# Trunk layer on one core: the experts' outputs are summed in DRAM by accumulating scatters

## The reference, cut to what matters

```python
_, idx = lax.top_k(jnp.where(emask, sel, -jnp.inf), TOP_K)
w = jnp.take_along_axis(scores, idx, axis=-1)
w = w / jnp.sum(w, axis=-1, keepdims=True) * ROUTED_SCALE          # 2.5
def block(args):                                                   # 128 slots of one expert
    tok, g, e = args
    xb = t_pad[tok]
    hb = jax.nn.silu(xb @ wg[e]) * (xb @ wu[e])
    return (hb @ wd[e]) * g[:, None]
out = jnp.zeros((T + 1, D), yb.dtype).at[slot_tok].add(yb.reshape(P, D))
...
return (routed + shared).reshape(B, L, D)
x = x + (gate_f * moe_ffn(h, p))                                   # then rmsnorm(x, g_final)
```

## Time and profile before

| | before |
|---|---|
| median of three runs | 2329.45 us |
| the profiled execution: time, span | 2326.84 us, 2325.0 us |
| PE busy in the span | 1948.6 us (84%) |
| DVE (VectorE), ACT (ScalarE), POOL (GpSimd) busy | 790.7, 330.1, 640.5 us |
| mean granted clock of PE | 0.918 |
| read from and written to HBM | 343.39 MB, 45.47 MB |

### The profile page before, as it was taken

One profiled execution on the slowest core, in us unless ns is written; L12 is line 12 of the kernel. 1 busy time (PEld: TensorE's weight loads), 2 busy tenths in 40 slices (PEclk: granted clock), 3 DMA queues, 4 the chain that ended last, 5 costly groups with the idle time before them and its releaser, 6 DMA issues. The chain is left out here.

```text
span 2325.0 us, 23841 instructions
## 1 busy us (share of the span) xinstructions
PE 1948.6 (84%) x7395; PEld 1099.0 (47%) x7396; DVE 790.7 (34%) x1150; ACT 330.1 (14%) x654; POOL 640.5 (28%) x853
## 2 busy tenths in 40 slices
PE   6999836888852567999998885999999999999965
PEld 3555415888841454555553452444444444444422
DVE  1000182444443962111111582333233232332336
ACT  2000232111114220000000110111111111111100
POOL 0000003333302210000000134455555555555444
PEclk8999957999975788999999977999999999999988
DMA  9442100000000014111114003999988999699656
GB/s 351 173 167 73 58 0 3 1 1 1 1 3 0 0 48 174 58 66 56 64 60 126 28 10 125 311 338 349 356 286 284 338 336 338 229 330 332 236 190 246
DMA packets 207419, 357.27 MB, mean 154 GB/s; under 512 B 24333, under 2 KB 158137, under 8 KB 203778
## 3 DMA queue, kind: packets, MB, share of 16 engines
q1 hardware_dynamic: 176338, 293.22, 36.6%
q0 software_dynamic: 31024, 63.27, 7.6%
HBM read 343.39 MB, written 45.47 MB: 167 GB/s over the span
## 5 line engine op out<-in xcount | busy, mean ns | idle before, releaser
L1853 PE MATMUL ps_gu_b<-we_gu,xgT 128*128 x1120 | 497.9, 598 | 39.9 <-issue 21.8
L1853 PEld LDWEIGHTS ps_gu_b<-we_gu,xgT 128*128 128x128 f32 x1120 | 208.1, 191 | 304.1 <-issue 304.1
L1806 POOL DMA_INDIRECT xg<-h_dram,idx_x x288 | 293.1, 1018 | 109.0 <-issue 109.0
L1276 PE MATMUL ps_logit<-hT_back,w_merge_tiles 128*128 128x512 f32 (+1 forms) x1024 | 284.4, 436 | 19.3 <-DMA w_merge_tiles<-w_merge 19.3
L1879 PE MATMUL ps_y_b<-we_dn,hsT_b 128*128 x560 | 253.2, 594 | 2.8 <-issue 2.8
L1276 PEld LDWEIGHTS ps_logit<-hT_back,w_merge_tiles 128*128 128x128 f32 x1024 | 158.1, 192 | 142.9 <-issue 123.5
L309 PE MATMUL ps_turn_and_in<-hT,w_tiles 128*128 128x512 f32 x704 | 197.8, 441 | 1.2 <-DVE hT L256 1.2
L1962 DVE TENSOR_TENSOR hs_b<-sg_b,ps_gu_b 128x256 f32<-128x256 f32 x70 | 29.4, 421 | 472.5 <-ACT sg_b L1911 451.7
L1879 PEld LDWEIGHTS ps_y_b<-we_dn,hsT_b 128*128 128x128 f32 x560 | 103.3, 190 | 120.8 <-issue 120.7
L309 PEld LDWEIGHTS ps_turn_and_in<-hT,w_tiles 128*128 128x128 f32 x704 | 108.8, 193 | 100.4 <-issue 100.4
L1953 DVE STREAM_TRANSPOSE xgT<-xg 128x1024 f32<-128x1024 f32 x72 | 145.1, 2015 | 15.0 <-DMA xg<-h_dram,idx_x 15.0
(11 more groups left out here) (411 smaller groups left out, 2214.0 us busy)
## 6 DMA issues: line engine op xcount, KB each, us to landing
we_gu<-we_gate SPq DMA_DIRECT2D x64, 1024.0 KB
we_gu<-we_up SPq DMA_DIRECT2D x64, 1024.0 KB
we_dn<-we_down SPq DMA_DIRECT2D x128, 512.0 KB
wmod<-w_mod SPq DMA_DIRECT2D x24, 1024.0 KB, 5.7
w_merge_tiles<-w_merge SPq DMA_DIRECT2D x32, 640.0 KB
w_tiles<-w_mix SPq DMA_DIRECT2D x22, 512.0 KB, 3.4
xg<-h_dram,idx_x POOLq DMA_INDIRECT x288
proj<-w_out SPq DMA_DIRECT2D x1, 4096.0 KB
```

Source lines behind the costliest of these rows:

```text
L1276: pe.matmul(ps_l[:, b, lo:hi], w[:, b, k * P:(k + 1) * P], hT[:, k, lo:hi], start=(k == 0), stop=(k == KD - 1))
L1806: pool.indirect_dma_start(xg[:, b, q, :], None, quarters, bass.IndirectOffsetOnAxis(ap=idx_x[:, b, q:q + 1], axis=0), bounds_check=4 * T - ...
L1853: mm = pe.matmul(ps_gu[:, b, :], xT[:, b, k].rearrange("p q s -> p (q s)"), w_gu[:, bass.ds(half[b], 1), k, :].rearrange("p a n -> p (a n) ...
```

## The change

- A list entry is now a pair: token number and the bits of its weight. Both are scattered at once, 8 bytes a row. The expert stage takes the two apart, turns both by a transpose, and the weight is multiplied in with the second SwiGLU product: a 128 x 1 copy and a multiply of three operands for each block (L1956, L1961).
- `y_dram` (5120 rows) is gone. `sum_dram` has a row per token (640). SP writes the shared expert's part there behind the first weight loads (L1777). A store adds its rows to it: the same scatter with `compute_op=ALU.add`, the row being the token number. Within a block all tokens differ.
- Between blocks they may not, so a store waits until the store of the other buffer has landed: `pool.wait_ge(y_store[1 - b], 16 * (i + b))`. Before the second lap's gathers GpSimd also waits for the shared part.
- The combining stage is `finish_tokens`: five plain loads of the sum, gate, residual, norm. Its outputs use one semaphore for each of two buffers.

```diff
-                            tok_u[:, t:t + 1], None).then_inc(scattered, 16)
+                            entry[:, t, j, :].bitcast(U32), None).then_inc(scattered, 16)
...
-                ch.link(dve.tensor_tensor_scan(end[:], ones[:, 0:N_EXP], cnt[:], 0.0, ALU.mult, ALU.add))
-                ch.link(dve.tensor_sub(base[:], end[:], cnt[:]))
-                take(c(B_ROW), base[:], c(B_EXPERT))
...
+                sp.dma_start(m.sum_dram.rearrange("(t p) d -> p t d", p=P), m.acc).then_inc(shared_out, 16)
                 with sp.Fori(1, n) as i:
                     pair(i)
...
                 def store(b, i, done):
                     for c in range(2):
                         pool.wait_ge(y_half_ok[c][b], i + 1)
+                    pool.wait_ge(y_store[1 - b], 16 * (i + b))
                     pool.wait_ge(pool_done, done)
...
-                    pool.indirect_dma_start(m.y_dram, bass.IndirectOffsetOnAxis(ap=idx_y[:, b, 0:1], axis=0),
-                                            y[:, b, :], None, bounds_check=T * TOP_K - 1, oob_is_err=False
+                    pool.indirect_dma_start(m.sum_dram, bass.IndirectOffsetOnAxis(ap=idx_y[:, b, 0:1], axis=0),
+                                            y[:, b, :], None, bounds_check=T - 1, oob_is_err=False, compute_op=ALU.add
                                             ).then_inc(y_store[b], 16)
                 for b in range(2):
                     gather(b, 0, 2 + 2 * b)
+                pool.wait_ge(shared_out, 16)
...
+                        dve.tensor_copy(w_col[:, b, :], all_w[:, bass.ds(2 * i + b, 1)]).then_inc(w_ok[b], 1)
...
-                        dve.tensor_mul(hs[:, b, :], hs[:, b, :], ps_gu[:, b, FF:]).then_inc(hs_ok[b], 1)
+                        dve.wait_ge(w_ok[b], i + 1)
+                        dve.scalar_tensor_tensor(out=hs[:, b, :], in0=hs[:, b, :], scalar=w_col[:, b, :],
+                                                 in1=ps_gu[:, b, FF:], op0=ALU.mult, op1=ALU.mult).then_inc(hs_ok[b], 1)
...
-def combine(nc, m):
+def finish_tokens(nc, m):
...
+                def residual(t):
+                    dve.wait_ge(moe_in[t], 16)
+                    ch.link(dve.tensor_mul(moe[:, t, :], moe[:, t, :], gate[:, group(t), :]))
+                    dve.tensor_add(m.x[:, t, :], m.x[:, t, :], moe[:, t, :]).then_inc(x_ok, 1)
+
+                dve.wait_ge(vec_in, 48)
+                residual(0)
                 for t in range(NT):
+                    if t + 1 < NT:
+                        residual(t + 1)
                     dve.wait_ge(sq_ok, t + 1)
```

More of the change, by code:

```diff
@@ L1364, in output_and_route @@
         pos_in, pos8, addr = a.sb("pos_in", [P, N_EXP]), a.sb("pos8", [P, NT, 8]), a.sb("addr", [P, NT, 8])
-        addr_u, tok_u = a.sb("addr_u", [P, NT, 8], U32), a.sb("tok_u", [P, NT], U32)
-        none_u = a.sb("none_u", [P, N_EXP * T // P], U32)
+        addr_u = a.sb("addr_u", [P, NT, 8], U32)
+        entry = a.sb("entry", [P, NT, TOP_K, 2])
+        weight = [entry[:, t, :, 1] for t in range(NT)]
+        none_u = a.sb("none_u", [P, 2 * N_EXP * T // P], U32)
         wsum = a.sb("wsum", [P, 1])
@@ L1370, in output_and_route @@
         used, count = a.sb("used_e", [P, N_EXP]), a.sb("count_e", [P, N_EXP])
-        ordinal, pairs, last, offset = (a.sb(n, [P, 1]) for n in ("ordinal", "pairs_e", "last_e", "offset_e"))
+        ordinal, pairs, last = (a.sb(n, [P, 1]) for n in ("ordinal", "pairs_e", "last_e"))
         tab = a.sb("tab", [P, TAB], I32)
@@ L1702, in _ @@
                 ch.link(dve.tensor_copy(m.list_row[:], last[:]))
[L1703 to L1709, removed]
+                for t in range(2, NT):
+                    silu(t)
 def experts(nc, m):
     QW = D // 4
-    NO_ROW = 65536.0
     with Tools(nc, "experts") as a:
@@ L1845, in _ @@
                               start=True, stop=True)
[L1846 removed]
+                pe.transpose(ps_list[:, 1, 0:P], list_f[:], ident)
+                pe.transpose(ps_list[:, 1, P:2 * P], list_w[:], ident).then_inc(list_turn, 1)
                 def lap(i):
@@ L1937, in _ @@
                 for q in range(4):
[L1938 to L1943, removed]
+                    dve.tensor_copy(list_4[:, q], list_u[:, 32 * q:32 * q + 32, 0].unsqueeze(1).to_broadcast([P, 4, 32]))
+                dve.tensor_copy(list_w[:], list_u[:, :, 1].bitcast(F32))
+                dve.tensor_copy(list_f[:], list_u[:, :, 0]).then_inc(list_turn, 1)
                 dve.wait_ge(list_turn, 2)
@@ L1946, in _ @@
                                   ps_list[:, 0, :].rearrange("p (q r) -> p q r", q=4),
-                                  4.0, m.place[:, 1:2], ALU.mult, ALU.add)
-                dve.tensor_scalar(all_y[:, :, 0], ps_list[:, 1, 0:P], m.place[:, 0:1], None, ALU.add
-                                  ).then_inc(list_ok, 1)
+                                  4.0, m.place[:], ALU.mult, ALU.add)
+                dve.tensor_copy(all_w[:], ps_list[:, 1, P:2 * P])
+                dve.tensor_copy(all_y[:, :, 0], ps_list[:, 1, 0:P]).then_inc(list_ok, 2)
                 def turn(b, i):
@@ L1973, in _ @@
                     lap(i)
[L1976 to L1980 removed]
+def finish_tokens(nc, m):
+    with Tools(nc, "finish_tokens") as a:
+        moe = a.sb("moe_sum", [P, NT, D])
         gate = a.sb("gate_f", [P, 2, D])
         gf = a.sb("g_final_b", [P, D])
[L1983 to L1985 removed]
         sq, out = a.sb("sq_f", [P, D]), a.sb("out_f", [P, 2, D])
         ss, rms = a.sb("ss_f", [P, NT]), a.sb("rms_f", [P, NT])
[L1988 to L1991 removed]
+        moe_in, out_store = a.ring("f_moe_in", NT), a.ring("f_out_store", 2)
+        (vec_in, x_ok, ms_ok, sq_ok, rms_ok, out_ok, chain) = a.sems(
+            "f_vec_in", "f_x_ok", "f_ms_ok", "f_sq_ok", "f_rms_ok", "f_out_ok", "f_chain")
         with nc.Block() as block:
@@ L2044, in _ @@
                 ch = Chain(dve, chain)
+                def residual(t):
+                    dve.wait_ge(moe_in[t], 16)
+                    ch.link(dve.tensor_mul(moe[:, t, :], moe[:, t, :], gate[:, group(t), :]))
+                    dve.tensor_add(m.x[:, t, :], m.x[:, t, :], moe[:, t, :]).then_inc(x_ok, 1)
                 dve.wait_ge(vec_in, 48)
-                def diagonals(t):
-                    dve.tensor_mul(diag[:, t % 2], m.const[:, 0:P].unsqueeze(1).to_broadcast([P, ON_PE, P]),
-                                   m.weight[:, t, 0:ON_PE].unsqueeze(2).to_broadcast([P, ON_PE, P])).then_inc(diag_ok, 1)
-                diagonals(0)
-                diagonals(1)
-                for t in range(NT):
-                    acc = m.acc[:, t, :]
-                    for j in range(ON_PE, TOP_K):
-                        dve.wait_ge(got[j], 16 * (t + 1))
-                        dve.scalar_tensor_tensor(out=acc, in0=rows[:, j, :], scalar=m.weight[:, t, j:j + 1],
-                                                 in1=acc, op0=ALU.mult, op1=ALU.add).then_inc(added, 1)
-                        dve.wait_ge(added, t * (TOP_K - ON_PE) + j - ON_PE + 1)
-                    dve.wait_ge(used, (t + 1) * ON_PE)
-                    if t + 2 < NT:
-                        diagonals(t + 2)
-                    dve.tensor_add(acc, acc, ps[:, t % 2, :]).then_inc(summed, 1)
-                    dve.wait_ge(summed, t + 1)
-                    ch.link(dve.tensor_mul(acc, acc, gate[:, group(t), :]))
-                    dve.tensor_add(m.x[:, t, :], m.x[:, t, :], acc).then_inc(x_ok, 1)
+                residual(0)
+                for t in range(NT):
+                    if t + 1 < NT:
+                        residual(t + 1)
                     dve.wait_ge(sq_ok, t + 1)
@@ L2122, in trunk_kernel @@
                 merge_branches(nc, m)
-            m.weight = whole.sb("weight", [P, NT, TOP_K])
-            m.y_row = whole.sb("y_row", [P, NT, TOP_K], U32)
             m.list_row = whole.sb("list_row", [P, 1], U32)
-            m.place = whole.sb("place", [P, 3])
+            m.place = whole.sb("place", [P, 1])
             m.laps = whole.sb("laps", [P, 2], I32)
```

81 lines of the change are left out of this document (25 added, 56 removed).

## The result

The changed kernel takes 2369.51 us (median of 4 runs, 2366.51 to 2375.27), the kernel before 2329.19 us beside it: ratio 1.018, 95% interval 1.0158 to 1.0202. The forecast was 2306 us, faster; the change went the other way. The time lies inside the wide range of 2270 to 2380 us, and rival 2 (GpSimd's wait, 2379 us) comes nearest to it.

A forecast was written before the change was run, and what follows sets the result against it. PE was taken to set the 22.1 us lap, DMA engines close behind. 2325.0 - 53.0 + 4 + 26 = 2302 us of span, plus 1.8 and 2.6, gave 2306 us; own range 2288 to 2324, 8 in 10 2270 to 2380.

The forecast's parts named there:

- rival 2: Store 1's wait for store 0 makes GpSimd's queue the bound: 3.8 us a lap, 99 us, 2379 us; chance 0.32.
- The tail: Combining stage: 92.4 us become 39.4 us (12.9 to g_final, 23.0 VectorE, 3.5 last output), a gain of 53.0 us.
- The end of the expert stage: Last store waits for the one ahead and lands more slowly itself: 4 us more, between 0 and 10.
- The laps: Expert loop: store 1 waits for store 0's landing of 7.8 us, period 23.1 us, 26 x 1.0 = 26 us.
- The nine other laps: Expert laps with the DMA queue all but empty: landing nearer 2.1 us, no loss.
- Rival 3: DMA engines become the bound in full laps: 0.8 us a lap, or 2.7 us, 70 us, 2350 us; chance 0.10.
- The rule cited: Adding stores: an add in the DMA path needs two source reads on one ring, halving the rate; the add costs nothing.
- The rest: VectorE's copies, routing and list entries: 0; shared part landing at about 1455, ahead of the second lap's gathers: at most 5 us.

The follow-up runs named there:

- e3: The kernel before with one line added, each store's wait for the landing of the other buffer's store, stores still plain: 2353.16 us, ratio 1.012.
- e2: The changed kernel with GpSimd's order store 0, four gathers, store 1, four gathers, the gathers one lap further ahead: 2315.38 us, ratio 0.9951.
- e12: e5 with every plain scatter issued twice, the second time into an array that nobody reads: 2318.45 us, ratio 0.9965.
- e9: e2 with gate and up weights laid out so a partition's 8 KB of one matrix lie together, same bytes: 2283.60 us, ratio 0.9815.
- e4: The changed kernel with a plain scatter in place of the adding one, all waits kept: 2298.89 us, ratio 0.9882.
- e5: e2 with a plain scatter in place of the adding one, order and waits kept: 2276.23 us, ratio 0.9784.
- e6: The changed kernel without the loads of further experts' weights, every block using the first two experts': 2278.31 us, ratio 0.9787.

## Why the prediction was wrong

- **The tail** (39.4 us, gain 53.0): right, 35.9 us and 56.5. Its parts 12.9 + 23.0 + 3.5 came as 11.2 + 21.1 + 3.5.
- **The end of the expert stage** (+4, 0 to 10): from the last issue to the next stage are 10.9 us against 6.4, and the wait ahead of it is 3.0 us against 1.3; with the longer issue some 7 us.
- **The laps** (26 x 1.0 us): the step that failed. They cost 89.3 us from the first store 0 to the last, against 26. "Period is 15.3 us + landing" holds in its form: the lap shown has 1.64 + 7.84 us from the issue of store 0 to the end of the wait, and 15.6 us for the rest. The forecast had 8.1 (landing 7.8, wake 0.3) and 15.0. So the landing was 1.4 us too short and the own work 0.6 us, the longer issue of the adding store 1, which I had set like a plain one. The full laps cost 2.9 us each and not 1.0, 75.5 us.
- **The nine other laps** were put at nothing, "the landing is nearer 2.1 us, no loss". The eight of them that lie between two stores cost 13.8 us. No add landed under 4.4 us, and in the lap from 2069.46, the lightest of them, the median was 6.2 us; in the four that lost time store 1 came 9.1 to 10.7 us after store 0, as in the full laps.
- **The number 26 itself** is near what the wait costs with a plain store (e3: 26.6 us), and that is in part luck: by the prediction's own sum a plain landing of 7.3 us gives 0.5 us a lap, 13 us. e3's full laps cost 0.8 us each, 20.7 us, and the rest falls elsewhere. As a plain landing the gathers' was a good guide (7.1 guessed, 7.3 measured). What was mis-sized is the add: "the destination is read once more for it ... 0.7 us" took one more read at a gather's rate for the whole price. In the landing it was about 1.4 us. Where the wait is covered the add still costs 39 us, which the sum left out.
- **Rival 3** had a chance of 0.10 "against it: ... PE waited for a weight load hardly ever although the engines were as busy". That is no argument: engines busy for 0.99 of a lap with nobody waiting have next to nothing left to give. Its milder form, 0.8 us a lap, would be 21 us in 26 laps; e2 shows 39.
- **The rule cited** from the Trainium skill, "Collectives: The Full Stack", section "The bandwidth ceiling: the fold count and why AG ≠ RS ≠ AR" (two source reads on one ring, the rate halved), is stated there for the reduce step of a collective and was carried over to this scatter. e12 agrees in the size, since two plain scatters cost what one add costs (2318.5 against 2315.4 us); that two reads are the reason, no run shows. The prediction took it for nearly neutral because it priced the read against a dip of 1.1 us in one lap.
- **Rival 2** was right in place (store 1's wait for store 0) and sign, and near in time (2379). Its point of decision, a landing of 8.7 us, was passed with 9.0. That the time came so near is luck: it took a landing of 10.6 us in 26 laps, and by its own sum 9.0 us would give 2.2 us a lap, 2337 us. The longer issue and the losses in the other laps made up for it.
- **The rest**: the shared part landed later than 1455; GpSimd waited 9.6 us, until 1458, and no lap shows a loss. VectorE's two small copies: nothing.

PE's clock falls too, by windows over laps of the changed kernel (columns as in the earlier trace rows):

```profile
1893.50:1918.80 25.30, 21.41 (x52) 9.37 (x52) 7.17 (x11) 2.73 (x6) 13.07 (x19) 0.99 1.02 322
1868.70:1893.50 24.80, 23.87 (x52) 10.32 (x53) 7.25 (x11) 2.73 (x6) 12.72 (x18) 0.90 0.89 280
...
1969.04:1994.12 25.08, 23.06 (x52) 10.02 (x52) 7.25 (x11) 2.73 (x6) 12.91 (x19) 0.93 0.88 284
1994.12:2019.23 25.11, 21.39 (x52) 9.38 (x52) 7.32 (x12) 2.73 (x6) 12.90 (x19) 1.00 0.99 318
```

The lap from 1868.70 began after a wait of 4.05 us, and the mean granted clock in it is 0.90, so PE ran for a part of it at 1.2 GHz and not at 2.4: its first 28 matmuls took 14.76 us in place of 12.28, and the lap's PE work 23.87 in place of 21.41. Over the whole group of gate and up matmuls this is 527.0 - 497.9 = 29 us. It is no second loss on top of the wait. The laps with the lower clock are no longer than the others, because GpSimd's period sets them and PE's longer work fills what would be idle time. GpSimd waited for y only 12.7 us in five times in the changed kernel, against 204.3 us in 68 before; the slower PE can hardly have cost the laps more than that.

## What to carry to other kernels

When a dependence on a landing enters an in-order queue, write down the queue's own work plus the landing, and compare it with the loop's period; if it doesn't fit, put other work of that queue between the two ends (e2: 54 us won by the order alone). Charge an accumulating scatter as two plain ones on the DMA engines, as it was here, and take a DMA share of 0.99 with nobody waiting for a full resource and not a free one. If the engines are the bound, look at the size of the packets before the number of bytes (e9). And if one queue's period is over PE's, a fall of PE's clock need not cost anything more.

## What the runs showed of the hardware

- An adding scatter of a block takes 1.62 us to issue where the plain one takes 1.04, and the small copy issued after it 0.75 us in place of 0.20.
- The same 181 MB of loads took 76.1% of the engines' time in packets of which most are under 2 KB, and 67.4% in a quarter as many packets; no PE time was lost by reading the 512 columns as two pieces of 256 (597 ns in e9, 598 before).
- The landing of an adding store in the changed kernel does not depend on how the weights are laid out (9.0 us, and 9.1 with wide loads), but it does on whether they are loaded at all (6.2 us without). A plain store's landing beside the same loads was 7.6 us with two stores in a row (e4) and 4.6 us with gathers between them (e5).
- What the packets of a queue take as a share of the engines depends on what runs beside them: in the 700 us from 1500, 21.1% for 34.5 MB beside the weight loads (changed kernel), 28.2% for 38.4 MB without them (e6).
